# Large SBUF tiles placed at multiples of 128 bytes in a three-layer mixer kernel

## The reference

```python
h = h + rms_norm(mixer(rms_norm(h, g0)), g1)
h = h + rms_norm(ffn(rms_norm(h, g2)), g3)
```

## Time and profile before

| what | before |
|---|---|
| median of 3 runs (lowest, highest) | 1204.3 us (1203.85, 1208.6) |
| profiled execution, its own time | 1204.32 us |
| its span, first to last instruction | 1202.5 us |
| granted TensorE clock, mean over the span | 1.00 |
| TensorE matmul busy | 1176.9 us, 98% |
| TensorE weight loads busy | 1076.7 us, 90% |
| VectorE busy | 847.2 us, 70% |
| ScalarE busy | 651.3 us, 54% |
| GpSimd busy | 151.4 us, 13% |
| DMA packets of the SP queue, share of 16 engines | 43.1% |

### The profile page before, as it was taken

How to read it: one execution, slowest core, us unless ns; L and a number is a source line. 1 busy time by engine, 2 the same in 40 slices (tenths; PEclk the granted TensorE clock), 3 DMA queues, 4 the chain that set the end, 5 groups by cost and what they waited for, 6 DMA issues and landing times.

```text
span 1202.5 us, 23183 instructions
## 1 busy us (share of the span) xinstructions
PE 1176.9 (98%) x9852; PEld 1076.7 (90%) x9852; DVE 847.2 (70%) x1299; ACT 651.3 (54%) x1171; POOL 151.4 (13%) x143
## 2 busy tenths in 40 slices
PE   8999999999999999999999999999999999999998
PEld 8897789999889898978999988999989878999986
DVE  6677777888557988886788874857577776655542
ACT  4657556666446665644666653665435534644431
POOL 1320000000002332101000000103443311000000
PEclk9999999999999999999999999999999999999999
DMA  8842225565625443353755564442222322755540
GB/s 308 268 141 89 98 101 207 192 210 194 231 106 176 151 182 141 114 184 105 259 196 181 206 245 158 178 176 106 107 107 71 120 93 92 277 196 190 184 167 35
DMA packets 31622, 196.67 MB, mean 164 GB/s; under 512 B 4000, under 2 KB 5664, under 8 KB 9376
## 3 DMA queue, kind: packets, MB, share of 16 engines
q1 hardware_dynamic: 27504, 185.17, 43.1%
q10 hardware_dynamic: 4016, 10.03, 2.6%
HBM read 193.09 MB, written 1.05 MB: 161 GB/s over the span
## 4 chain that ended last, share of the span: by engine, by line
PE 88%; DVE 5%; ACT 3%; issue 2%; POOL 1%; DMA 0%; DVEq 0%; POOLq 0%; ACTq 0%
PE bank L538 24%; PE bank L540 24%; PE bank L539 24%; DVE wlo L527 2%; PE bank L1894 1%; PE bank L1132 1%; PE bank L1189 1%; PE bank L1216 1%; ACT whi L519 1%; PE bank L725 1%; PE bank L2538 1%; PE bank L3005 1%; PE bank L2481 1%; POOL rr L667 0%; PE bank L2525 0%
## 5 line engine op out<-in xcount | busy, mean ns | idle before, releaser
L527 DVE TENSOR_TENSOR wlo<-raw,whi 128x1024 fp32r<-128x1024 f32 x322 | 389.0, 1245 | 87.9 <-ACT whi L519 87.3
L538 PE MATMUL bank<-xT,wlo 128*128 128x256 f32 x1488 | 418.6, 281 | 4.2 <-DVE wlo L527 2.1
L539 PE MATMUL bank<-xT,whi 128*128 128x256 f32 x1488 | 413.1, 278 | 0.0
L540 PE MATMUL bank<-xT,whi 128*128 128x256 f32 x1488 | 413.1, 278 | 0.0
L519 ACT ACTIVATE whi<-raw 128x1024 fp32r<-128x1024 f32 (+1 forms) x349 | 349.2, 1048 | 115.9 <-PE bank L540 86.7
L538 PEld LDWEIGHTS bank<-xT,wlo 128*128 128x128 f32 x1488 | 279.5, 188 | 7.9 <-DVE xc L1601 2.8
L539 PEld LDWEIGHTS bank<-xT,whi 128*128 128x128 f32 x1488 | 279.6, 188 | 0.6 <-issue 0.5
L540 PEld LDWEIGHTS bank<-xT,whi 128*128 128x128 f32 x1488 | 279.4, 188 | 0.0
L667 POOL TENSOR_TENSOR rr<-rr,nhalf 128x1 f32<-128x1 f32 x34 | 24.7, 729 | 710.0 <-DVE rr L655 522.4
L538 PE MATMUL bank<-whi,gT 128*128 128x512 f32 x264 | 104.6, 396 | 0.0
L540 PE MATMUL bank<-whi,gT 128*128 128x512 f32 x264 | 104.4, 395 | 0.0
(11 more groups left out here) (390 smaller groups left out, 1766.5 us busy)
## 6 DMA issues: line engine op xcount, KB each, us to landing
raw<-in_wall SPq DMA_DIRECT2D x173, 1024.0 KB, 4.8
grow<-in_rows ACTq DMA_DIRECT2D x13, 512.0 KB, 5.3
h<-in_x SPq DMA_DIRECT2D x4, 256.0 KB, 5.3
dsk<-in_rows ACTq DMA_DIRECT2D x4, 256.0 KB, 3.4
memx<-in_mem ACTq DMA_DIRECT2D x1, 1024.0 KB, 10.5
out<-h SPq DMA_DIRECT2D x4, 256.0 KB, 2.0
masks<-in_masks SPq DMA_DIRECT2D x1, 580.0 KB, 13.3
D<-Tx ACTq DMA_DIRECT2D x4, 128.0 KB, 5.8
```

Source lines behind the costliest of these rows:

```text
L527: e.tensor_tensor(low, src, high, SUB).then_inc(*up("dve.low", p))
L538: e.matmul(out, a[1], b[0], start=start, stop=False)
L539: e.matmul(out, a[0], b[1], start=False, stop=False)
L540: return e.matmul(out, a[0], b[0], start=False, stop=stop)
```

## The change

Only the order and the sizes of tile declarations change; no instruction is moved, added or removed. In `root` the order becomes raw, whi, wlo, h, xT, sqj, xs, grow, grow2, masks, identb, negb, cols, valid, srow, nhalf, ss, rr, and an unused tile that fills up to the next multiple of 128. masks is widened by 24 floats, X by 28 floats each (the zeroed end `X[i][:, 960:XW]` grows with it). kcz moves to the end of the attention's tiles, and the small tiles of the delta rule's stage move behind the large ones.

```diff
-        cols = sb([128, _NCOL], name="cols")
-        masks = sb([128, _MASKS], name="masks")
+        h = sb([128, 2, 1024], name="h")
+        xT = [sb([128, 8, 256], f32r, name="xT") for _ in range(2)]
+        sqj = sb([128, 1024], name="sqj")
+        xs = sb([128, 1024], name="xs")
+        grow = sb([128, 1024], name="grow")
+        grow2 = sb([128, 1024], name="grow2")
+
+        masks = sb([128, _MASKS + 24], name="masks")
+        identb = sb([128, 128], bf16, name="identb")
         negf_w = 2 * 128 + 64 + 30 + 8 + 4 + 1
         negb = sb([128, negf_w - 1], bf16, name="negb")
-        identb = sb([128, 128], bf16, name="identb")
+        cols = sb([128, _NCOL], name="cols")
         valid = sb([128, 2], name="valid")
         srow = sb([128, 32 + 32 + 16], name="srow")
-        grow = sb([128, 1024], name="grow")
         nhalf = sb([128, 1], name="nhalf")
-        h = sb([128, 2, 1024], name="h")
-        xT = [sb([128, 8, 256], f32r, name="xT") for _ in range(2)]
         ss = sb([128, 8], name="ss")
         rr = sb([128, 4], name="rr")
-        sqj = sb([128, 1024], name="sqj")
-        xs = sb([128, 1024], name="xs")
-        grow2 = sb([128, 1024], name="grow2")
+        room = -nc.sbuf_base % 128 // 32
+        if room:
+            sb([128, 8 * room], name="room")
...
-        kcz = sb([128, 4, 15], st=nsa, name="kcz")
         Tx = sb([128, 1024], st=nsa, name="Tx")
...
-        XW = 16 * 60 + 68
+        XW = 16 * 60 + 96
...
+        kcz = sb([128, 4, 15], st=nsa, name="kcz")
         nsa.close()
...
         ygT = [sb([128, 12, 256], f32r, gd, "yG") for _ in range(2)]
+        kT2, qT2, vT2, zt2 = ([sb([128, 2, 256], st=gd, name="pj") for _ in range(2)] for _ in range(4))
+        ma = ExitStack()
+        qmT = sb([128, 4, 256], st=ma, name="qmT")
...
+        ma.close()
+        ctx = []
...
+        for c in ctx:
+            c["eqk"], c["rqk"] = (sb([128, 8], st=gd, name="eqk") for _ in range(2))
+            c["brk"], c["kek"], c["sk"], c["ro"] = (sb([128, 4], st=gd, name="sm") for _ in range(4))
         beta = sb([128, 2, 8], st=gd, name="beta")
...
```

More of the change, by code:

```diff
@@ L428, in build @@
         ygT = [sb([128, 12, 256], f32r, gd, "yG") for _ in range(2)]
+        kT2, qT2, vT2, zt2 = ([sb([128, 2, 256], st=gd, name="pj") for _ in range(2)] for _ in range(4))
+        ma = ExitStack()
+        qmT = sb([128, 4, 256], st=ma, name="qmT")
+        mP = [sb([128, 512], st=ma, name="mP") for _ in range(2)]
+        mPT = [sb([128, 512], st=ma, name="mPT") for _ in range(2)]
+        ym = sb([128, 2, 512], st=ma, name="ym")
+        mnmx = [sb([128, 4], st=ma, name="mnmx") for _ in range(2)]
+        msum = sb([128, 2, 4], st=ma, name="msum")
+        ma.close()
+        ctx = []
+        for i in range(2):
+            c = {n: sb([128, 4, 128], st=gd, name=n) for n in ("kbg", "kg", "vb")}
+            c["Ct"] = [sb([128, 4, 64], st=gd, name="Ct") for _ in range(2)]
+            c["LY"] = sb([128, 2, 4, 64], st=gd, name="LY")
+            c["TU"] = sb([128, 2, 4, 64], st=gd, name="TU")
+            c["PT"] = sb([128, 4, 64], st=gd, name="PT")
+            c["LT"], c["Ym"] = c["LY"][:, 0, :, :], c["LY"][:, 1, :, :]
+            c["vn"], c["wT"], c["oi"] = c["vb"], by_128(c["LY"]), by_128(c["TU"])
+            c["S"] = c["Ct"][0][:, :, :].rearrange("p a b -> p (a b)").rearrange("p (a b) -> p a b", a=2)
+            ctx.append(c)
+        for c in ctx:
+            c["eqk"], c["rqk"] = (sb([128, 8], st=gd, name="eqk") for _ in range(2))
+            c["brk"], c["kek"], c["sk"], c["ro"] = (sb([128, 4], st=gd, name="sm") for _ in range(4))
         beta = sb([128, 2, 8], st=gd, name="beta")
@@ L437, in build @@
         Ag = sb([128, 8], st=gd, name="Ag")
[L438 to L459, removed]
         DT = xs[:, :].rearrange("p (h t n) -> p h t n", h=8, t=2)
```

## The result

The changed kernel takes **1221.99 us** (median of 4 runs, 1221.71 to 1222.25), beside 1206.45 us for four runs of the kernel before (1203.85, 1204.3, 1208.6 and 1211.88). The ratio is 1.0131, with an interval of 1.0109 to 1.0152: slower by 1.3%, clear of noise. The profiled execution took 1222.25 us with a span of 1220.4, against 1204.32 and 1202.5 before: 17.9 us more. The experiments show why single runs of the kernel before lie on levels some 4 us apart.

What follows compares the result with a forecast made beforehand. TensorE, busy 98% of 1202.5 us, was taken as the bound. Terms of 18.3, 3.8 and 2.6 us made 24.7; half of the last two's 6.4 counted, 21.5 on 1204.3 gave 1226. Range 1194 to 1232, the forecast's own 1216 to 1232.

Steps and rivals of the forecast that it cites:

- The forecast case: 256-column matmuls on xT slow to mT's pace, chiefly in the up-projections: 21.5 us slower, 1226 us; chance 0.50.
- (1): VectorE and ScalarE: copies and norm reads take the same time at either offset; nothing.
- (2): DMA loads of grow and grow2: landing may shift by 3.2 us either way, once; taken as 0.
- (3): Small matmuls: transposes keep their pace, the 320 products of 64x64 change under 1 us; taken as 0.
- The rival without an effect: Pace on TensorE is fallen into after a stall, not set by addresses: 1204 us; no effect or under 6 us, 0.22.
- The faster rival: Aligned moving xT keeps the fast pace everywhere or beats it: 1194 us (0.16) or 1176 us (0.12), together 0.28.
- (4): 512-column matmuls, weights moving over gT or xT: same pace, 232 to 233 ns, so taken as 0.
- (5): 256-column matmuls on xT take mT's pace: 18.3 us in up-projections, 3.8 us elsewhere moving, 2.6 us stationary; 24.7 us.
- The half of 6.4 us: xT's matmuls outside the up-projections' long runs and stationary xT: waits shorten, so half of their 6.4 us counted.
- The high end's 123 ns: Upper bound: 123 ns in place of 120 on 864 more matmuls, 2.6 us, with all 24.7 us: 1231.6.
- mT and the 512-column rows stay as they are: Sign for the profile after: mT's matmuls and the 512-column matmuls keep their durations while xT's slow.
- its own test: The reading is wrong if mT's pace changes while its offset doesn't: a chance pace was read.

Runs made afterwards that it cites:

- e9: The kernel before with srow declared behind xT, so that xT moves to distance 0 from the weights and the stages stay: 1227.21 us, 1.0192.
- e4: The kernel before with 64 unused bytes ahead of raw, so that every tile moves by 64 and distances between tiles stay: 1203.99 us, 1.0001.
- p3: The kernel before plus 20 unread blocks of 48 matmuls at five distances, behind one to four transposes: 120.0 ns at 0, both 113.3 and 117.8 at 64.
- e7: The kernel before with one transpose issued once more ahead of each up-projection's long run, no address changed: 1215.91 us, 1.0072.
- e2: The kernel before with 128 unused bytes behind grow2, so that only the stage tiles (gT, yT, yG, mT) move: 1201.09 us, 0.9962.
- e1: The kernel before with ss and rr declared ahead of xT, so that xT moves to distance 128 and the stages stay: 1221.99 us, 1.0147.
- e8: The changed kernel with xT 64 bytes past the weights again, plus a doubled transpose ahead of each up-projection's long run: 1210.04 us, 1.0023.
- e3: The changed kernel with xT put 64 bytes past the weights again, the stages kept at distance 0: 1209.73 us, 1.0048.
- p1: The kernel before plus unread blocks of 45 matmuls with 256 moving columns at each distance: 113.3 to 120.0 ns with 128 stationary columns.
- p2: The kernel before plus unread blocks of 30 matmuls with 512 moving columns at each distance: 226.6 to 236.7 ns with 128 stationary columns.
- e10: The kernel before with 128 unused bytes between h and xT, putting xT 64 bytes to the weights' other side, stages at distance 0: 1200.95 us, 0.9968.

## Why the prediction was right, and where its steps were not

**Right.** The forecast case came: xT at 120.0 ns in all three up-projections, medians of 283 within the stated 281 to 286, and the largest term, 2736 x 6.7 ns = 18.3 us, to the tenth. e9, which moves xT and leaves the stages, gave 22.8 us against the 21.5 worked out. Steps (1), (2) and (3) were right to what can be measured: the norms' rows and the 64x64 products stand, and in e4 every tile moves at no cost. The rival without an effect is out as the cause of the slowing: at distance 0 xT has 120.0 ns in all six up-projections of the two traces (after, e9), and gT in all four blocks of p3. Its mechanism, a pace that the streams fall into, is real all the same: e7 moves the time by it with no address changed. The faster rival is out as well: its condition was that the start of the moving operand counts, and e4 moved it to a multiple of 128 for nothing.

**The step that failed** is (4), "the same pace, 232 to 233 ns, so no effect of the stationary tile's offset [...] Taken as 0". It compared gT with xT, distances 128 and 64 modulo 256, which happen to have the same 512-column pace, and took the offsets modulo 128, in which gT, yT, yG and mT don't move. They moved by 128 bytes because `root` ends 128 bytes later. The term taken as 0 was worth -7.0 us: 6.5 us on gT, yT and yG, which e2 moves without xT, and 0.5 us on the 96 over xT. That is more than the 4 us by which 1226 lies above 1222; without it 1226 would have been low (e9: 1227). That it is so near is in part luck, as errors of both signs cancel.

**Mis-sized in (5):** xT stationary, "864 x 3 = 2.6 us", measured 4.3 ns and 3.7 us, since the earlier trace rows average 113.5 and 117.9 where I took 116 and the pace after is 119.8, not 119. The half of 6.4 us that waits were to absorb was too much: in e9 the rows add to 24.3 us (25.6 less 0.5 over xT and less 0.8 for gT, yT and yG, which were a little faster than before) and 22.8 were measured, so 1.5 us were absorbed and not 3.2. The high end's 123 ns, "286 less 163", took one line for all: on mT's three lines the medians were 286, 281 and 284, at 120.0 ns from start to start.

**mT.** "mT and the 512-column rows stay as they are" failed for both. The average pace of mT was 120.0 before and after, but on its lines 286 became 283, and mT's distance had changed, from 128 to 0. The forecast rested on it for the wrong reason: xT at mT's old distance gives 118.7 (e1), not 120.0. And the 120.0 was only one of two paces of mT at that distance: in e1, which doesn't touch mT, it has 118.7. The forecast came to the right value because distance 0 has 120.0 too, and that is luck. By its own test ("I am wrong if mT's own pace changes while its offset doesn't: then a chance pace, and not the offset, was what I read"), which e1 meets, the reading was wrong, though the time was right.

**The page's rule.** The traces show one shape with 113.3 to 120.0 ns at one granted clock, and e1 and e9 slow it by moving tiles alone. The Trainium skill, SBUF — State Buffer, section Who interferes with whom, by which TensorE's two reads don't wait on each other, would have given 0 here and differs from e1, e2, e9 and both probes. The lower price by the formula of the Trainium skill, TensorE: Matmul & The Clock Gate, section Wait — 56ns, not 53.3ns?, an estimate of 109 and 216 ns, was met by none of them: the least for this type is 113.3 and 226.6.

**Open.** What settles which of two paces a stretch takes was not found: e8 and e3 fall to 117.8 each time, e2 mostly to 113.3, with xT at the same distance. Why mT at distance 128 has 120.0 in some kernels and 118.7 in e1, why 144 fails under xT and gT with the weights at 112, and what in TensorE or the memory makes distance 0 slow for 256 columns and fast for 512, are open too. That it is a conflict between the stationary load and the moving read is not shown: p1's 32-column groups speak for it, p2's at distance 0 against it.

**A version that beats both** is e2: the kernel before and 128 unused bytes behind grow2, 0.9962 (0.9948 to 0.9976); e10 equals it with 0.9968.

## What to carry to other kernels

When TensorE is the bound and never idle, read its pace from start to start by stage before touching tile placement: what was worth tuning here is the distance between stationary and moving tiles modulo 256 (0 for 512 moving columns, 64 or 192 for 256), and not the alignment of each to 128 bytes, which was worth nothing. Any tile added or resized ahead of others shifts the distances of all behind it, so work out the addresses modulo 256 of every pair that meets in a matmul, also of those "left alone". A run of matmuls may hold one of two paces from its start on, so a change of a few instructions ahead of it can move the time by 1% though they themselves take 0.1 us; compare the paces first.

## What the runs showed of the hardware that was not expected

- The pace of a 128x128 float32r matmul at 2.4 GHz (granted clock 1.00) was 113.3 to 120.0 ns with 256 columns and 226.6 to 236.7 ns with 512, by where its operands lie and, at 64 and at 128 bytes apart, by which of two paces a stretch falls into.
- Distance 0 is the slowest with 256 columns (120.0) and, with 144, the fastest with 512 (226.6 and 226.7). With 32 stationary columns in place of 128 it is faster with 256 moving columns (117.7) and slower with 512 (231.8).
- With xT 64 bytes from the weights the same instructions run at 113.3 or 117.8 ns for 912 matmuls on end (both in one execution of e10); one transpose more ahead of each of the three stretches (e7) cost 12 us beside the traced run of before, and runs of one kernel lie on levels 4.1 us apart, which is one such stretch.
